# Half of the expert scatter issued inside the down products, and half of its adds issued ahead of the scatter weights

## The chip, the core and the metric

One core of one Trainium2 chip runs the whole program. The metric is device time in microseconds (us), the median of several executions. Engines: PE is TensorE, DVE is VectorE, ACT is ScalarE, POOL is GpSimd, SP is SyncE, which here issues the weight transfers.

## The reference

One decoder layer over T = 320 tokens (256 of a prompt, 8 sequences of 8) with D = 1024: adaLN modulation, an input projection, two gated linear recurrences, their merge and output projection, and then a mixture of experts, top 4 of 32. In float32:

```python
h2 = rmsnorm(x, n2) * (1 + sc2) + sh2
top_v, top_i = lax.top_k(h2 @ r_w + r_b, 4)      # softmax over the four
for e in range(32):
    gu = h2 @ w_gu[e] + b_gu[e]                  # w_gu[e]: 1024 x 2048
    gate, up = min(gu[:, :1024], 7), clip(gu[:, 1024:], -7, 7)
    act = (up + 1) * (gate * sigmoid(1.702 * gate))
    out += combine[:, e:e+1] * (act @ w_dn[e] + b_dn[e])   # w_dn[e]: 1024 x 1024
y = rmsnorm(x + gt2 * out, final_g)
```

## The kernel before

Everything ahead of the experts is as it was and is not touched. Each expert's tokens are cut into items of at most 32 tokens (CAP). In the profiled execution there are 56 items for 32 experts, each expert with one, two or three. PE, ACT and DVE each run a loop over items; SP runs a loop over experts and only issues transfers.

**Weights.** An expert has 12 slots of 1 MB: slots 0 to 7 hold rows of w_gu, slots 8 to 11 two blocks of w_dn each. Slots 3 to 11 have one buffer in the ring, so the transfer for expert e waits until the last item of expert e-1 has used the slot (L434, on slot_used; L431 on gu_ready; L433 on dn_ready). Slots 0 to 2 have two buffers (ring for even experts, late for odd ones). Transfers go out in the order of the slots.

**One item on PE** (item, L835 to L872), in the order of its queue:

1. bias (L842, four matmuls) and the gate/up products (L848, eight blocks k of four matmuls, each for 32 of the array's columns, written 128*32 in the profile), block k after slot k has landed;
2. gather(i + 1) (L802), which picks the next item's tokens by a selection matrix;
3. scatter of the first half (L818, n = 0 to 3): it takes the down result of the item before (dng) and its scatter weights (SelWT) and spreads the 32 rows over the 320 tokens. Each n is one matmul on 32 rows of the array (32*128), and the four of a half lie on the four row groups; they go to banks 4, 5, 6, 7;
4. two transposes of the activations (L858) after act_ready, and two of the gathered tokens (L809);
5. scatter of the second half (n = 4 to 7), to the same four banks. Matmul n waits until DVE has added bank n - 4 into yacc (pe.wait_ge on summed, L817);
6. the wait for act_copied, the down products (L867, eight blocks of four matmuls, 128*32), then three transposes of the next scatter weights (L824, flip_weights).

A float32 matmul is two instructions on PE, so a group of four matmuls stands as 8.

**One item on DVE** (L1508 to L1521): select (L1496), the clamped activation (L1512 to L1516, which sets act_ready), three operations for the scatter weights SelW (L1518), one for the bias selection (L1501), and then add_scattered, eight adds of 320 columns, one for each bank (L1506).

**One item on ACT** (L1090 to L1099): sigmoid (L1092), copies of the gathered tokens (L1080), of the flipped activations actT (L1095, sets act_copied), of the flipped tokens (L1084), of the down result dng (L1098, after dn_ready) and of the scatter weights (L1088).

After the last item PE scatters the last down result (L925) and DVE scales yacc and adds it to xT (L1537 to L1550).

Of the kernel before, what the change touches and what calls it, by code (L numbers as in the profile page):

```python
# [48 lines left out]
GRP = P // CAP  # L49
# [119 lines left out]
def build(nc, a):  # L169
    ctx = ExitStack()  # L170
    with ctx:
# [46 lines left out]
        def cut(at, n):  # L218
            return bigv[:, at:at + n]
# [3 lines left out]
        def units(ap, n):  # L223
            return ap.rearrange("p (u t) -> p u t", u=n)
# [4 lines left out]
                 k=units(cut(3 * HT, HT), 4), kd=units(cut(4 * HT, HT), 4), qs=units(cut(5 * HT, HT), 4)),  # L229
# [10 lines left out]
        def C(name, rows=P):  # L240
            at, n = CONST_COLS[name]
            return consts[0:rows, at:at + n]
# [118 lines left out]
        def item_slot(s):  # L361
            return (SLOT0 + s) % NSLOT
# [4 lines left out]
        def item_buffer(s, odd):  # L367
            return late[:, s * SLOT:(s + 1) * SLOT] if odd and s < NAHEAD else ring[:, item_slot(s), :]

        def pair(n):  # L370

            return ring[:, n % NSLOT, :].rearrange("p (k c) -> p k c", k=2)
# [7 lines left out]
        FEATURES = [2 * (n % GRP) + n // GRP for n in range(DC)]  # L380
# [138 lines left out]
        def _(pe):  # L519
# [266 lines left out]
            def chunk(k):  # L786

                at = (k % 2) * P + (k // 2) * CAP
                return slice(at, at + CAP)

            def part(g):
                return slice(CAP * g, CAP * g + CAP)

            def columns(g):
                return slice(HALF * g, HALF * g + HALF)

            def gather(j):

                pe.wait_ge(sel_ready, j + 1)
                for p in range(3):  # L800
                    for g in range(GRP):
                        last = mm(banks[0][part(g), 0:HALF], Sel[:, p, :], h2tok[:, p, columns(g)],  # L802
                                  start=(p == 0), stop=(p == 2), tile_position=(0, CAP * g))
                last.then_inc(gathered, 1)

            def flip_gathered(j):
                pe.wait_ge(gtok_copied, j + 1)
                for x in range(2):
                    last = nc.tensor.transpose(banks[0][:, HALF + x * P:HALF + (x + 1) * P], gtok[:, x * P:(x + 1) * P], ident)  # L809
                last.then_inc(gtok_flipped, 1)  # L810

            def scatter(i, fills):

                for n in fills:
                    x, g = n // GRP, n % GRP
                    if n >= GRP:
                        pe.wait_ge(summed, i * 8 + (n - GRP + 2))  # L817
                    mm(banks[SCATTER[n]][:, 0:T], dng[part(g), x * P:(x + 1) * P], SelWT[part(g), :],  # L818
                       start=True, stop=True, tile_position=(CAP * g, 0)).then_inc(scattered, 1)

            def flip_weights(j):
                pe.wait_ge(selw_ready, j + 1)
                for p, (t0, tn) in enumerate(TILES):
                    last = nc.tensor.transpose(banks[3][:, t0:t0 + tn], SelW[0:tn, p, :], ident[0:tn, 0:tn])  # L824
                last.then_inc(selw_flipped, 1)

            def wait_weights(s, pairs, odd):
                if s >= NAHEAD:
                    pe.wait_ge(slot_landed[item_slot(s)], pairs * 32 + (16 * odd + item_landed_count(s)))
                elif odd:  # L830
                    pe.wait_ge(late_landed[s], pairs * 16 + 16)
                else:
                    pe.wait_ge(slot_landed[item_slot(s)], pairs * 16 + item_landed_count(s))

            def item(i, pairs, odd):  # L835

                pe.wait_ge(h2g_copied, i + 1)
                pe.wait_ge(bsel_ready, i + 1)
                out = banks[1][:, :].rearrange("p (m c) -> p m c", m=2)
                bias = bgu.rearrange("p (m c) -> p m c", m=2)  # L840
                for g in range(GRP):
                    mm(out[part(g), :, :], bsel[0:96, :], bias[0:96, :, columns(g)], start=True, stop=False,  # L842
                       tile_position=(0, CAP * g))
                for k in range(DC):
                    wait_weights(k, pairs, odd)
                    w = item_buffer(k, odd).rearrange("p (m c) -> p m c", m=2)
                    for g in range(GRP):
                        last = mm(out[part(g), :, :], h2g[:, chunk(k)], w[:, :, columns(g)], start=False, stop=(k == DC - 1),  # L848
                                  tile_position=(0, CAP * g))
                    last.then_inc(gu_ready if k == DC - 1 else slot_used, 1)  # L850
                gather(i + 1)
                pe.wait_ge(dn_copied, i + 1)
                pe.wait_ge(selw_copied, i + 1)
                pe.wait_ge(summed, i * 8 + 1)
                scatter(i, range(GRP))
                pe.wait_ge(act_ready, i + 1)
                for x in range(2):
                    last = nc.tensor.transpose(banks[2][:, x * P:(x + 1) * P], actb[:, x * P:(x + 1) * P], ident)  # L858
                last.then_inc(act_flipped, 1)
                flip_gathered(i + 1)  # L860
                scatter(i, range(GRP, 2 * GRP))
                pe.wait_ge(act_copied, i + 1)
                for k in range(DC):
                    if k % 2 == 0:
                        wait_weights(DC + k // 2, pairs, odd)
                    for g in range(GRP):
                        last = mm(banks[2][part(g), HALF:2 * HALF], actT[:, chunk(k)],  # L867
                                  pair(item_slot(DC + k // 2))[:, k % 2, columns(g)],
                                  start=(k == 0), stop=(k == DC - 1), tile_position=(0, CAP * g))
                    if k % 2:  # L870
                        last.then_inc(dn_ready if k == DC - 1 else slot_used, 1)
                flip_weights(i + 1)  # L872

            X = NI
# [38 lines left out]
            with pe.Fori(0, E // 2) as pairs:  # L913
                e = pairs * 2
                n0, n1, n2 = first_item(e), first_item(e + 1), first_item(e + 2)
                with pe.Fori(n0, n1) as i:
                    item(i, pairs, False)
                with pe.Fori(n1, n2) as i:
                    item(i, pairs, True)
# [198 lines left out]
        def _(dve):  # L1118
# [371 lines left out]
            def col(tab, p, j):  # L1490
                return tab[:, p, j:j + 1] if isinstance(j, int) else tab[:, p, ds(j, 1)]

            def select(j):

                for p in range(3):
                    ins = TS(Sel[:, p, :], C("slot_no")[:, 0:CAP], col(posI, p, j), None, ALU.is_equal)  # L1496
                ins.then_inc(sel_ready, 1)

            def select_bias(j):
                c = OHI[0:96, j:j + 1] if isinstance(j, int) else OHI[0:96, ds(j, 1)]  # L1500
                TS(bsel[0:96, :], ones[0:96, 0:CAP], c, None, ALU.mult).then_inc(bsel_ready, 1)  # L1501

            def add_scattered(i):
                for n, f in enumerate(FEATURES):
                    dve.wait_ge(scattered, i * 8 + (n + 1))
                    TT(yacc[:, f, :], yacc[:, f, :], banks[SCATTER[n]][:, 0:T], ALU.add).then_inc(summed, 1)  # L1506

            def item(i):  # L1508
                dve.wait_ge(gathered, i + 1)
                select(i + 1)  # L1510
                dve.wait_ge(gu_ready, i + 1)
                TS(gbuf, banks[1][:, 0:HALF], LIMIT, None, ALU.min).then_inc(gate_clamped, 1)  # L1512
                step(TS(ubuf, banks[1][:, HALF:2 * HALF], -LIMIT, LIMIT, ALU.max, ALU.min))  # L1513
                step(STT(ubuf, ubuf, 1.0, gbuf, ALU.add, ALU.mult))  # L1514
                dve.wait_ge(swish_ready, i + 1)
                TT(actb, ubuf, sbuf_, ALU.mult).then_inc(act_ready, 1)  # L1516
                for p in range(3):
                    ins = TS(SelW[:, p, :], C("slot_no"), col(posI, p, i), col(wI, p, i), ALU.is_equal, ALU.mult)  # L1518
                ins.then_inc(selw_ready, 1)
                select_bias(i + 1)  # L1520
                add_scattered(i)  # L1521

            PER_ITEM = 2
            n0 = S.n
# [1 line left out]
            with dve.Fori(0, count) as i:  # L1526
                S.base = i * PER_ITEM
                item(i)
                assert S.n == n0 + PER_ITEM
# [72 lines left out]
```

## Time and profile before

| what | value |
|---|---|
| time, median of 3 runs | 1543.33 us (1541.24 to 1546.66) |
| the profiled execution's own time | 1542.54 us |
| its span, first to last instruction | 1540.7 us |
| PE busy | 1397.3 us, 91% |
| DVE busy | 523.0 us, 34% |
| ACT busy | 275.0 us, 18% |
| mean granted TensorE clock | 0.932 |
| first item starts / last item's L824 ends | 460.88 / 1518.10 us |

The row of the span and the row of the time differ by 1.8 us that lie outside the first and the last instruction. The items take 1057 of the 1541 us. A busy PE is not a PE at its peak: the ends of matmuls are modelled and the clock changes.

### The profile page before, as it was taken

The page shows a single profiled execution, that of the slowest core. Times are in us where ns is not written, and L with a number is a line of the kernel's source. Part 1 is how long each engine was busy: PE and PEld are TensorE (multiplying, and loading weights), DVE is VectorE, ACT ScalarE, POOL GpSimd, SP SyncE. Part 2 cuts the span into 40 slices and gives each one's busy share as a digit, 9 for nine tenths or more (in the row PEclk, how much of TensorE's full clock was granted, in tenths as well). Part 3 has the DMA queues.
Part 4 walks back from the last instruction along what each step waited for, and adds up shares of the span by engine and source line. Part 5 has one row for each costly group of instructions (what it writes and reads, how often), then busy time and mean ns, then how long its engine had stood idle before and what let it go on. Part 6 is the DMA issues. An engine that isn't in the chain of part 4 may idle for free.

```text
span 1540.7 us, 30155 instructions
## 1 busy us (share of the span) xinstructions
PE 1397.3 (91%) x11837; PEld 668.9 (43%) x11838; DVE 523.0 (34%) x1490; ACT 275.0 (18%) x517; POOL 22.8 (1%) x38
## 2 busy tenths in 40 slices
PE   5999999999969997988798999898999789899996
PEld 2656666666743442433242443333344223344443
DVE  3133342333463341323242433333334223333335
ACT  2120021010021121211111222121221112122222
POOL 0000010000000000000000000000000000000000
PEclk9999989788979999999798999999999989999998
DMA  9777342013348899999999989997899999985760
GB/s 391 304 289 272 140 166 109 16 51 132 91 178 330 350 388 418 410 408 420 416 411 410 388 356 386 417 412 287 327 379 375 417 418 412 410 358 208 291 245 34
DMA packets 87448, 470.77 MB, mean 306 GB/s; under 512 B 7984, under 2 KB 8000, under 8 KB 51360
## 3 DMA queue, kind: packets, MB, share of 16 engines
q1 hardware_dynamic: 84416, 460.68, 73.8%
q0 software_dynamic: 2432, 7.75, 1.9%
q10 hardware_dynamic: 576, 2.00, 0.3%
q8 instruction: 17, 0.28, 0.1%
q14 instruction: 7, 0.06, 0.0%
HBM read 465.56 MB, written 4.85 MB: 305 GB/s over the span
## 4 chain that ended last, share of the span: by engine, by line
PE 70%; DMA 15%; DVE 8%; issue 4%; SPq 2%; DVEq 1%; ACT 0%
PE bank L848 21%; PE bank L867 12%; PE bank L600 11%; DMA ring<-in_exp_w_gu 8%; PE bank L818 7%; DMA ring<-in_exp_w_dn 6%; PE bank L732 2%; PE bank L747 2%; SPq L442 2%; PE bank L598 2%; PE bank L824 2%; DVE gates L1506 1%; DVE big L1514 1%; DVE big L1518 1%; DVE big L1513 1%
## 5 line engine op out<-in xcount | busy, mean ns | idle before, releaser
L848 PE MATMUL bank<-ring,big 128*32 128x512 f32 x2840 | 351.0, 633 | 49.1 <-DMA ring<-in_exp_w_gu 48.8
L1512 DVE TENSOR_SCALAR big<-bank 128x256 f32<-128x256 f32 x56 | 23.8, 425 | 705.3 <-PE bank L848 705.3
L867 PE MATMUL bank<-ring,big 128*32 128x256 f32 x3584 | 221.8, 401 | 3.8 <-DMA ring<-in_exp_w_dn 3.8
L848 PEld LDWEIGHTS bank<-ring,big 128*32 128x32 f32 x2840 | 84.5, 113 | 287.2 <-issue 169.4
L818 PE MATMUL bank<-big 32*128 32x320 f32 x912 | 161.9, 481 | 26.6 <-DVE gates L1506 25.0
L1506 DVE TENSOR_TENSOR gates<-gates,bank 128x320 f32<-128x320 f32 x448 | 182.7, 477 | 1.5 <-PE bank L818 1.5
L600 PE MATMUL bank<-late,ring 128*128 128x320 f32 (+1 forms) x592 | 177.4, 461 | 3.9 <-DVE late L1166 3.1
L867 PEld LDWEIGHTS bank<-ring,big 128*32 128x32 f32 x3584 | 115.6, 115 | 107.5 <-issue 39.8
L600 PEld LDWEIGHTS bank<-late,ring 128*128 128x128 f32 (+1 forms) x592 | 117.3, 201 | 68.8 <-issue 27.5
L818 PEld LDWEIGHTS bank<-big 32*128 32x128 f32 x912 | 84.9, 183 | 82.6 <-DVE gates L1506 38.3
L1092 ACT ACTIVATE big<-big 128x256 f32<-128x256 f32 x56 | 23.4, 417 | 452.3 <-DVE big L1512 452.3
L848 PE MATMUL bank<-late,big 128*32 128x512 f32 x744 | 87.0, 598 | 3.9 <-DMA late<-in_exp_w_gu 3.9
L802 PE MATMUL bank<-vtok,big 128*32 128x256 f32 x1368 | 88.5, 395 | 1.4 <-DVE big L1451 1.4
L1098 ACT ACTIVATE big<-bank 128x256 f32<-128x256 f32 x56 | 21.5, 384 | 335.3 <-PE bank L867 335.3
L802 PEld LDWEIGHTS bank<-vtok,big 128*32 128x32 f32 x1368 | 44.3, 115 | 64.3 <-issue 44.9
L1092 ACT ACT_TABLE_LOAD x56 | 71.8, 1283 | 1.1 <-issue 0.2
L1518 DVE TENSOR_SCALAR big<-consts,big 128x128 f32<-128x128 f32 x168 | 47.8, 341 | 0.1
L842 PE MATMUL bank<-big 96*32 96x512 bf16 x224 | 22.6, 392 | 22.2 <-issue 22.2
L848 PEld LDWEIGHTS bank<-late,big 128*32 128x32 f32 x744 | 22.0, 109 | 46.5 <-issue 36.0
L732 PE MATMUL bank<-gates,ring 128*128 128x320 f32 x128 | 37.6, 459 | 0.6 <-DVE gates L1361 0.6
L824 PE MATMUL bank<-consts,big 128*128 128x128 f32 x171 | 36.9, 293 | 0.0
L548 PE MATMUL bank<-ring,Sst 128*32 128x512 f32 x192 | 25.5, 672 | 12.3 <-DVE Sst L1127 6.5
(265 smaller groups left out, 945.2 us busy)
## 6 DMA issues: line engine op xcount, KB each, us to landing
ring<-in_exp_w_gu SPq DMA_DIRECT2D x208, 1024.0 KB, 11.4
ring<-in_exp_w_dn SPq DMA_DIRECT2D x128, 1024.0 KB, 11.2
late<-in_exp_w_gu SPq DMA_DIRECT2D x48, 1024.0 KB, 15.4
ring<-in_ada_w SPq DMA_DIRECT2D x24, 1024.0 KB, 20.6
ring<-in_w_in SPq DMA_DIRECT2D x20, 1024.0 KB, 9.7
ring<-in_w_out SPq DMA_DIRECT2D x4, 1024.0 KB, 7.4
ring<-in_w_in SPq DMA_DIRECT2D x4, 528.0 KB, 10.1
late<-in_state_hgrn POOLq DMA_DIRECT2D x4, 512.0 KB, 7.6
```

The source lines that it names most:

```text
L442: sp.dma_start(dst, src).then_inc(late_landed[s] if ahead and odd else slot_landed[item_slot(s)], 16)
L598: ins = mm(b[0:tn, :], hT[:, k, t0:t0 + tn], wts, start=(k == 0), stop=(k == DC - 1))
L600: ins = mm(b[0:w, 0:T], wts, hT[:, k, :], start=(k == 0), stop=(k == DC - 1))
L732: ins = mm(b[:, 0:T], pair(s0 + k // 2)[:, k % 2, f * P:(f + 1) * P], gates[:, 4 * bi + k, :], start=(k == 0), stop=(k == H - 1))
L802: last = mm(banks[0][part(g), 0:HALF], Sel[:, p, :], h2tok[:, p, columns(g)], start=(p == 0), stop=(p == 2), tile_position=(0, CAP * g))
L818: mm(banks[SCATTER[n]][:, 0:T], dng[part(g), x * P:(x + 1) * P], SelWT[part(g), :], start=True, stop=True, tile_position=(CAP * g, 0)).the ...
L824: last = nc.tensor.transpose(banks[3][:, t0:t0 + tn], SelW[0:tn, p, :], ident[0:tn, 0:tn])
L848: last = mm(out[part(g), :, :], h2g[:, chunk(k)], w[:, :, columns(g)], start=False, stop=(k == DC - 1), tile_position=(0, CAP * g))
L867: last = mm(banks[2][part(g), HALF:2 * HALF], actT[:, chunk(k)], pair(item_slot(DC + k // 2))[:, k % 2, columns(g)], start=(k == 0), stop= ...
L1092: A(sbuf_, gbuf, ACT.Sigmoid, scale=ALPHA).then_inc(swish_ready, 1)
L1506: TT(yacc[:, f, :], yacc[:, f, :], banks[SCATTER[n]][:, 0:T], ALU.add).then_inc(summed, 1)
L1518: ins = TS(SelW[:, p, :], C("slot_no"), col(posI, p, i), col(wI, p, i), ALU.is_equal, ALU.mult)
```

## The change

The second half of the scatter leaves its place ahead of the down products and is issued after block k = 3 of the eight. add_scattered is cut in two: the adds of n = 0 to 3 come directly after the activation, ahead of the scatter weights; the adds of n = 4 to 7 stay at the end. No operation is added or removed, and the semaphores count as before.

```diff
                 last.then_inc(act_flipped, 1)
                 flip_gathered(i + 1)
-                scatter(i, range(GRP, 2 * GRP))
                 pe.wait_ge(act_copied, i + 1)
                 for k in range(DC):
...
                     if k % 2:
                         last.then_inc(dn_ready if k == DC - 1 else slot_used, 1)
+                    if k == 3:
+                        scatter(i, range(GRP, 2 * GRP))
                 flip_weights(i + 1)
...
-            def add_scattered(i):
-                for n, f in enumerate(FEATURES):
+            def add_scattered(i, x):
+                for n in range(GRP * x, GRP * x + GRP):
+                    f = FEATURES[n]
                     dve.wait_ge(scattered, i * 8 + (n + 1))
                     TT(yacc[:, f, :], yacc[:, f, :], banks[SCATTER[n]][:, 0:T], ALU.add).then_inc(summed, 1)
...
                 TT(actb, ubuf, sbuf_, ALU.mult).then_inc(act_ready, 1)
+                add_scattered(i, 0)
                 for p in range(3):
                     ins = TS(SelW[:, p, :], C("slot_no"), col(posI, p, i), col(wI, p, i), ALU.is_equal, ALU.mult)
                 ins.then_inc(selw_ready, 1)
                 select_bias(i + 1)
-                add_scattered(i)
+                add_scattered(i, 1)
```

## Rows read from the trace of the kernel before

**Rows 1.** The page: chain of work that ended last, by engine.

```profile
PE 70%; DMA 15%; DVE 8%; issue 4%; SPq 2%; DVEq 1%; ACT 0%
```

**Rows 2.** The stretches of items: length, busy of each engine, PEclk, DMA share, GB/s.

```profile
564.25:625.10 60.85, 52.16 (x538) 20.91 (x538) 18.53 (x57) 10.69 (x21) 0.00 (x0) 0.94 0.97 398
...
686.17:777.18 91.01, 76.30 (x718) 27.75 (x718) 24.59 (x76) 14.26 (x28) 0.00 (x0) 0.87 1.01 414
...
1179.32:1270.22 90.90, 74.82 (x718) 27.49 (x717) 24.78 (x76) 14.26 (x28) 0.00 (x0) 0.89 0.98 399
1270.22:1330.97 60.75, 53.27 (x538) 21.37 (x538) 18.44 (x57) 10.69 (x21) 0.00 (x0) 0.92 1.01 414
460.88:564.25 103.37, 99.05 (x1075) 42.82 (x1076) 37.02 (x114) 19.67 (x40) 0.00 (x0) 0.97 0.89 360
...
1061.49:1179.32 117.83, 112.06 (x1255) 48.83 (x1255) 43.02 (x133) 24.95 (x49) 0.00 (x0) 1.00 0.82 333
1330.97:1518.10 187.13, 179.44 (x1970) 77.70 (x1969) 70.51 (x214) 39.21 (x77) 0.00 (x0) 0.98 0.65 264
```

**Rows 3.** Timeline of one item: start, us, engine, line, operation, [idle before <- what ended it].

```profile
906.92 0.40 PE L842 MATMUL bank<-big 96*32 96x512 bf16 x4
...
907.15 7.04 PE L848 MATMUL bank<-ring,big 128*32 128x512 f32 x64
...
915.41 0.82 PE L818 MATMUL bank<-big 32*128 32x320 f32 x8
915.52 0.42 DVE L1516 TENSOR_TENSOR big<-big 128x256 f32<-128x256 f32 x1
...
915.86 0.85 DVE L1518 TENSOR_SCALAR big<-consts,big 128x128 f32<-128x128 f32 x3
916.16 0.20 PEld L858 LDWEIGHTS bank<-consts,big 128*128 128x128 f32 x2 [0.44 <-DVE big L1516]
...
916.64 0.38 ACT L1095 ACTIVATE big<-bank 128x256 f32<-128x256 f32 x1 [0.70 <-PE bank L858]
916.78 3.26 DVE L1506 TENSOR_TENSOR gates<-gates,bank 128x320 f32<-128x320 f32 x8
...
917.30 1.99 PE L818 MATMUL bank<-big 32*128 32x320 f32 x8 [0.48 <-DVE gates L1506]
...
919.23 3.66 PE L867 MATMUL bank<-ring,big 128*32 128x256 f32 x64
...
922.82 0.64 PE L824 MATMUL bank<-consts,big 128*128 128x128 f32 x3
...
923.39 0.40 PE L842 MATMUL bank<-big 96*32 96x512 bf16 x4
```

**Rows 4.** Timeline of PE alone, from just before the first scatter.

```profile
915.09 0.39 PE L802 MATMUL bank<-vtok,big 128*32 128x256 f32 x4
```

**Rows 5.** Transfers: one SP issue in order of time.

```profile
568.29 3.76 SPq L442 DMA_DIRECT2D ring<-in_exp_w_gu  x5
```

**Rows 6.** Chain of waits over the span: down products, first and last longer one.

```profile
507.75 5.28 PE bank L867 x64
...
1446.37 5.28 PE bank L867 x64
```

**Rows 7.** Windows before and in one of those down products (columns as Rows 2).

```profile
503.90:507.70 3.80, 3.32 (x27) 1.89 (x23) 3.77 (x13) 1.04 (x3) 0.00 (x0) 1.00 1.00 423
508.10:511.40 3.30, 3.30 (x38) 1.69 (x32) 0.83 (x4) 0.00 (x0) 0.00 (x0) 0.50 0.99 417
```

**Rows 8.** Timeline of PE in an item whose weights lag.

```profile
752.91 1.93 PE L848 MATMUL bank<-ring,big 128*32 128x512 f32 x8 [0.55 <-DMA ring<-in_exp_w_gu]
```

**Rows 9.** Timeline after the last item.

```profile
1514.71 0.69 DVE L1537 TENSOR_TENSOR gates<-gates,modT 128x512 f32<-128x512 f32 x1
...
1518.62 0.68 DVE L1541 TENSOR_TENSOR xT<-xT,gates 128x512 f32<-128x512 f32 x1
...
1519.80 0.22 DVE L1545 TENSOR_TENSOR gates<-bank,modT 128x64 f32<-128x64 f32 x1 [0.50 <-PE bank L818]
```

## The prediction

> **What bounds the kernel now.** I read the chain of waits first: PE has 70% of it and the DMA 15% [rows 1]. The items take 1057 of the 1541 us, and the change touches nothing else, so the question is in which items PE sets the pace and in which the weights do. For that I cut the items into stretches and took the windows of each [rows 2]. Eight stretches contain an expert with a single item: six of three items, 60.75 to 61.07 us long (first and last shown), and two of four items, 91.01 and 90.90 us. In these the DMA engines are 0.97 to 1.02 busy at about 400 to 414 GB/s. The other four stretches hold 30 items (6, 6, 7 and 11; three shown), where the DMA share is 0.65 to 0.93 and an item takes 16.47 us from one L842 to the next [rows 3]. There PE, and what it waits for, sets the pace.
>
> Inside such an item the timeline shows where PE does little. The first scatter takes 0.82 us for four matmuls side by side. The second takes 1.99 us for the same four, because each waits for an add (eight adds in 3.26 us, 0.41 apart), and the first add begins only after SelW and the bias selection, at 916.78. Meanwhile actT was ready at 917.02 (916.64 + 0.38), and the down products begin at 919.23 [rows 3].
>
> **The change in a PE-bound item.** All operations remain, 8 scatters and 8 adds.
>
> *Moved out:* the down products now wait for act_copied alone. ACT's copy ends at 917.02, and a semaphore takes about 0.05 us (the first add ends near 917.25, the scatter starts at 917.30), so they start at 917.08: 2.15 us earlier.
>
> *Moved in:* the scatter after k = 3. From the start of one group to the start of a scatter of the other tile shape took 0.32 us (L802 at 915.09, L818 at 915.41) [rows 3, 4]; the unpaced scatter takes 0.82; after the old one L867 started 0.07 before its modelled end; and the step to the next group that would have been there anyway, 0.22 (3.59 us for 16 groups), is deducted [rows 3]. That is 0.85, and I take 0.89 for the slower first step after a switch. The waits inside are satisfied and I cost them at nothing: L848 too waits for a slot before each of its eight blocks, and its 64 instructions run in 7.04 us without a gap [rows 3]. Their cover is that PE is busy with products while its queue runs ahead.
>
> *Are the waits really satisfied?* The first scatter's results are there at about 916.2 (915.41 + 0.80), so DVE stands idle 0.3 us after L1516 and then adds from 916.27 to 917.94. The scatter inside starts at 917.08 + 1.79 + 0.1 = 918.97. Its first matmul needs the first add (916.75), its last one the fourth (917.94): 1.0 us to spare. Queued on DVE behind the new waits are SelW (0.85, now ready near 918.8 instead of 916.7) and the bias selection (near 919.0). flip_weights wants SelW at 921.56 and the next L842 wants the bias near 922.1, so both are hidden by some 2.7 us. The second adds run from about 919.8 to 921.4, then select; the gather needs that 7 us later. ACT's order is unchanged. On SP the release of slots 8 and 9 comes 2.15 us earlier, and everything later 1.26 us; no wait is added and nothing stands behind one.
>
> So L824 starts at 917.08 + 3.59 + 0.89 = 921.56 instead of 922.82. An item saves 2.15 - 0.89 = **1.26 us** and takes 15.21.
>
> *Bounds of the insertion.* Below: without any cost of the switch, 0.65 (saves 1.5). Above: if the four matmuls follow one another at the old pace, 0.1 + 1.93 = 2.03 (saves 0.12). The nearest row is the first scatter, whose waits were satisfied and whose shape is the same, hence 0.89.
>
> A rule speaks against the change. The Trainium skill, TensorEngine Tiling (Array Packing), Key Properties, says that a change of tiling mode drains the engine, and the new order has one change of mode more. The rows put a switch at 0.1 us over a plain step (0.32 against 0.22). If the drain meant waiting for the last matmul's full 0.39 us, the insertion would be 0.96 and the saving 1.19 us: 2 us less over 30 items, which the range holds.
>
> **Where it does not arrive.** In the eight stretches the stream is already full. Each begins when the last item of an expert releases slot 3, about 4 us after its start (564.25 in [rows 2], 568.29 in [rows 5]), and ends when the last slot of the expert after the single one has landed. Faster PE work inside changes neither. I cost them at zero gain: 26 items x 1.26 = 33 us that are not received.
>
> In the PE-bound stretches a two-item expert comes close to the stream as well. One more expert adds 91.0 - 60.9 = 30.1 us; a three-item stretch less one expert leaves 30.75, and two new items take 30.42 [rows 2]. At seven changes of expert with no loop step of PE between them, about 0.3 us is lost: 2.2 us.
>
> **The clock.** Nine of the 56 down products take 5.28 instead of 3.59 us in the chain (first and last shown of the four in PE-bound stretches) [rows 6]. The granted clock in one of them was 0.50, that is 1.2 instead of 2.4 GHz, and just before PE had issued only 27 instructions in 3.8 us: transposes, the wait for the first add, the paced scatter [rows 7]. Those 3 sparse us shrink to about one. I expect these drops to vanish: 4 x 1.69 = 6.8 us (the other five fall in stream-bound stretches and are free).
>
> Against it: at the exit of a stream-bound stretch the down products now wait for their slots themselves (a slot lands every 2.5 us, 30.1 / 12, and has 0.9 us of products, so PE is a third busy). In such phases before, the clock stood at half for long, and a block took 1.93 us instead of 1.04 [rows 8]. If the last blocks and the next item's first ones meet such a spell, an exit costs about 1.7 us. I take half of the eight exits: 6.8 us given back; bounds 0 and 13.5.
>
> **The tail.** DVE ends its last adds now 0.7 us before the end of L824 instead of 3.4. Behind them stand L1537 to L1541: from 1514.71 to 1519.30. L1545 started at 1519.80 [rows 9], so 0.5 of the shift of 2.65 us is hidden and **2.1 us** are added.
>
> **Sum** against the profiled execution's 1542.5 us (span 1540.7 and 1.8 around it; the median of the runs, 1543.3, is 0.8 above): -30 x 1.26 = -37.8; +2.2 stream; -6.8 clock; +6.8 exits; +2.1 tail. Together -33.5, that is **1509 us**.
>
> **Rivals.**
>
> A. *The inserted scatter is not concurrent.* Four matmuls with a wait each could go one after another, 2.03 us. For: every scatter of this form with waits in the trace ran at 0.41 us each. Against: there the adds set exactly this pace. Saves 0.12 x 30 = 3.6 us, clock 6.8 gained, exits not worse, tail +2.1: about 1534. Halfway (insertion 1.4): about 1522. Decides from an insertion over 1.2.
>
> B. *Slower: the clock falls in the down products of every item.* A switch of tile shape in the middle with matmuls on 32 rows could leave a sparse phase in each item. For: half clock did follow the old scatter nine times. Against: 47 times it did not, and the phase is now denser. Price 1.69 for the products and 0.4 for the scatter against 1.26 saved: +0.8 x 30 = 25, tail 2: about 1569. It turns to slower from about three items in five.
>
> C. *The clock gets worse at the exits and the short drops stay.* Exits 13.5, no 6.8 won: about 1522.
>
> D. *The stream hides it anyway.* If the whole were stream-bound, nothing would change: 1543. Against it the DMA share of 0.65 to 0.93 in four stretches [rows 2].
>
> E. *Everything goes well:* no cost at the exits, insertion 0.65: -4 and -6.8, about 1498.
>
> **Chances.** Forecast, 1502 to 1516: 0.50; E 0.14; C 0.14; A with its halfway case 0.15 (fully 0.05); B 0.04; D 0.03. The range leaves out B, D, the full A and the lower part of E: 1496 to 1530. A measurement of this kernel tells about 0.3% (5 us) from nothing. Faster: all but B, D and a little of A, 0.92; same 0.03; slower 0.05.
>
> **What would show it.** Right: L867 starts some 0.05 us after ACT's L1095 ends in every PE-bound item, the second L818 takes 0.8 us between two parts of L867, the period is 15.2, and PE no longer idles before L818 for DVE's adds; the eight stretches keep 60.8 and 91.0 us. Wrong: a second L818 of 1.5 us or more (A); down products of over 7 us with a clock of 0.5 (B); stretches longer than before (C). The prediction fails if the down products find another late partner or if PE pays more than 0.9 us for the interruption.

## The result and the profile after

The changed kernel takes 1508.21 us (median of 4 runs, 1502.62 to 1510.14) against 1544.99 us for the kernel before beside it: a ratio of 0.9757, 95% interval 0.9721 to 0.9793. It is faster by 2.4%, and the forecast was 1509. A second series (changed_again below) gave 1507.68 us and 0.9777.

The profiled execution is the lowest of the four runs, 1502.6 us with a span of 1500.8. Its first item starts at 456.60 instead of 460.88 us. Nothing was changed ahead of the items, and in the other profiles of this study that start lies between 457.4 and 463.0 whatever the kernel, so 4.3 of its 39.9 us are not the change's. The items themselves go from 1057.2 to 1019.2 us, 38.0 less, and the tail after them from 22.6 to 25.0, 2.4 more.

The timeline of one item after (columns as in [rows 3]; lines have moved by a few, L866 was L867, L1096 was L1095, L1508 was L1506, L1518 was L1516):

```profile
915.15 0.82 PE L818 MATMUL bank<-big 32*128 32x320 f32 x8
915.25 0.42 DVE L1518 TENSOR_TENSOR big<-big 128x256 f32<-128x256 f32 x1
...
915.90 0.44 PE L858 MATMUL bank<-consts,big 128*128 128x128 f32 x2
915.99 1.68 DVE L1508 TENSOR_TENSOR gates<-gates,bank 128x320 f32<-128x320 f32 x4 [0.31 <-PE bank L818]
...
916.38 0.39 ACT L1096 ACTIVATE big<-bank 128x256 f32<-128x256 f32 x1 [0.69 <-PE bank L858]
...
916.82 1.93 PE L866 MATMUL bank<-ring,big 128*32 128x256 f32 x32 [0.26 <-ACT big L1096]
917.59 0.85 DVE L1521 TENSOR_SCALAR big<-consts,big 128x128 f32<-128x128 f32 x3
...
918.68 0.82 PE L818 MATMUL bank<-big 32*128 32x320 f32 x8
...
919.43 2.21 PE L866 MATMUL bank<-ring,big 128*32 128x256 f32 x32
919.52 1.68 DVE L1508 TENSOR_TENSOR gates<-gates,bank 128x320 f32<-128x320 f32 x4 [0.93 <-PE bank L818]
...
920.56 0.59 PEld L866 LDWEIGHTS bank<-ring,big 128*32 128x32 f32 x16 [0.55 <-DMA ring<-in_exp_w_dn]
```

This answers to [rows 3]. The down products start 0.05 us after ACT's copy ends (916.38 + 0.39) and wait 0.26 us for it. The second scatter, 1.99 us long before, is 0.82 long and lies between two parts of the products. DVE idles 0.31 us before its first four adds. A PE-bound item takes 15.21 us in place of 16.47. The item shown is the last of its stretch and took 15.48: the second part of its products is 2.21 us long instead of 1.93, because a slot of w_dn landed late (PEld at 920.56).

The windows of the stretches, same items as in [rows 2]:

```profile
core 0: us, PE busy (x) PEld busy (x) DVE busy (x) ACT busy (x) POOL busy (x), PEclk, DMA share, GB/s
554.45:616.55 62.10, 51.16 (x539) 17.90 (x538) 19.00 (x57) 10.69 (x21) 0.00 (x0) 0.92 0.99 405
677.38:768.18 90.80, 71.14 (x718) 23.16 (x717) 25.33 (x76) 14.26 (x28) 0.00 (x0) 0.89 1.01 415
...
1153.83:1244.77 90.94, 71.35 (x718) 23.01 (x718) 25.32 (x76) 14.26 (x28) 0.00 (x0) 0.89 1.00 412
1244.77:1305.54 60.77, 51.65 (x539) 18.07 (x538) 19.00 (x57) 10.69 (x21) 0.00 (x0) 0.89 1.01 414
456.60:554.45 97.85, 92.65 (x1074) 36.29 (x1074) 37.99 (x114) 19.67 (x40) 0.00 (x0) 0.98 0.92 375
1044.63:1153.83 109.20, 105.00 (x1255) 42.01 (x1254) 44.33 (x133) 24.95 (x49) 0.00 (x0) 1.00 0.86 349
1305.54:1475.84 170.30, 165.05 (x1970) 65.53 (x1969) 69.92 (x207) 39.20 (x77) 0.00 (x0) 1.00 0.71 290
```

The stretches with a single-item expert keep their length: 90.80 and 90.94 where 91.01 and 90.90 stood, 60.77 where 60.75 stood. Two have grown, the first by 1.25 us and the one from 922.14 to 983.81 (not shown) by 0.80. The other four gave all of the gain, 39.7 us (510.1 to 470.4). One of them, from 829.10 to 922.14 (not shown, 93.04 us), now has a DMA share of 1.00 itself. PE's busy share went down in the stream-bound ones: the saved work became waiting for weights.

The last items' tail answers to [rows 9]:

```profile
1475.14 0.69 DVE L1540 TENSOR_TENSOR gates<-gates,modT 128x512 f32<-128x512 f32 x1
1475.20 0.64 PE L824 MATMUL bank<-consts,big 128*128 128x128 f32 x3
...
1476.66 0.82 PE L818 MATMUL bank<-big 32*128 32x320 f32 x8 [0.82 <-ACT big L1089]
1479.04 0.69 DVE L1544 TENSOR_TENSOR xT<-xT,gates 128x512 f32<-128x512 f32 x1
1479.76 0.23 DVE L1548 TENSOR_TENSOR gates<-bank,modT 128x64 f32<-128x64 f32 x1
```

PE's last scatter ends at 1477.5 and DVE takes it up only at 1479.76, after its own queue. Before, it waited 0.50 us for PE at this place; now PE is ready 2.3 us earlier than DVE.

### The profile page after: what moved, and what is told of

Its sections match the earlier page's. It is cut to its first block, busy times and chain, and to the rows that moved or that the text cites. A ratio compares the mean times of both kernels' runs of the same rounds, so it can differ in the third digit from the quotient of the medians.

```text
span 1500.8 us, 30155 instructions
## 1 busy us (share of the span) xinstructions
PE 1336.0 (89%) x11837; PEld 604.8 (40%) x11838; DVE 533.0 (36%) x1490; ACT 275.0 (18%) x517; POOL 22.8 (2%) x38
## 4 chain that ended last, share of the span: by engine, by line
PE 68%; DMA 20%; SPq 6%; DVE 2%; issue 2%; ACT 1%; DVEq 0%
PE bank L848 19%; DMA ring<-in_exp_w_dn 17%; PE bank L600 12%; PE bank L866 10%; SPq L442 6%; PE bank L818 4%; PE bank L802 4%; PE bank L732 2%; PE bank L747 2%; PE bank L598 2%; DMA ring<-in_exp_w_gu 2%; PE bank L824 2%; DMA ring<-in_ada_w 1%; ACT big L1096 1%; PE bank L548 1%
## 5 line engine op out<-in xcount | busy, mean ns | idle before, releaser
L848 PE MATMUL bank<-ring,big 128*32 128x512 f32 x2840 | 358.1, 643 | 47.1 <-DMA ring<-in_exp_w_gu 47.1
L866 PE MATMUL bank<-ring,big 128*32 128x256 f32 x3584 | 221.6, 383 | 33.3 <-DMA ring<-in_exp_w_dn 18.5
L1508 DVE TENSOR_TENSOR gates<-gates,bank 128x320 f32<-128x320 f32 x448 | 188.3, 483 | 74.4 <-PE bank L818 74.4
L848 PEld LDWEIGHTS bank<-ring,big 128*32 128x32 f32 x2840 | 85.0, 114 | 295.9 <-issue 169.0
L600 PE MATMUL bank<-late,ring 128*128 128x320 f32 (+1 forms) x592 | 174.0, 454 | 3.1 <-DVE late L1167 3.1
L866 PEld LDWEIGHTS bank<-ring,big 128*32 128x32 f32 x3584 | 102.4, 109 | 137.0 <-DMA ring<-in_exp_w_dn 34.9
L1093 ACT ACTIVATE big<-big 128x256 f32<-128x256 f32 x56 | 23.4, 417 | 479.5 <-DVE big L1514 479.5
L848 PE MATMUL bank<-late,big 128*32 128x512 f32 x744 | 91.5, 613 | 20.0 <-DMA late<-in_exp_w_gu 20.0
L818 PE MATMUL bank<-big 32*128 32x320 f32 x912 | 96.1, 483 | 3.8 <-DVE xT L1551 3.0
L818 PEld LDWEIGHTS bank<-big 32*128 32x128 f32 x912 | 37.3, 184 | 51.4 <-issue 47.5
L842 PE MATMUL bank<-big 96*32 96x512 bf16 x224 | 22.6, 392 | 23.1 <-issue 23.1
L824 PE MATMUL bank<-consts,big 128*128 128x128 f32 x171 | 36.8, 293 | 0.0
## 6 DMA issues: line engine op xcount, KB each, us to landing
ring<-in_ada_w SPq DMA_DIRECT2D x24, 1024.0 KB, 20.6
```

Of the source, the lines that this page charges most:

```text
L600: ins = mm(b[0:w, 0:T], wts, hT[:, k, :], start=(k == 0), stop=(k == DC - 1))
L1093: A(sbuf_, gbuf, ACT.Sigmoid, scale=ALPHA).then_inc(swish_ready, 1)
```

## The experiments

Each profile was cut into the same stretches (from one L842 to the next). "Eight" are the stream-bound stretches together, 26 items, "four" the PE-bound ones, 30 items; both come from the one profiled execution. The item is one inside an expert whose weights do not lag. Each ratio is to executions of the kernel before beside that run, whose medians lie between 1542.67 and 1544.99 us.

| kernel | median us | ratio to before, 95% | item us | eight us | four us |
|---|---|---|---|---|---|
| before | 1544.99 | 1 | 16.47 | 547.1 | 510.1 |
| changed | 1508.21 | 0.9757 (0.9721 to 0.9793) | 15.21 | 548.9 | 470.4 |
| adds_ahead_only | 1521.72 | 0.9846 (0.9816 to 0.9877) | 15.96 | 547.5 | 489.5 |
| scatter_inside_only | 1507.89 | 0.9751 (0.9714 to 0.9788) | 15.21 | 549.1 | 472.0 |
| no_second_scatter | 1504.73 (one run) | | 14.32 | 551.3 | 468.2 |
| scatter_split | 1531.99 | 0.9912 (0.9886 to 0.9937) | 16.07 | 547.7 | 499.2 |
| scatter_after_k1 | 1504.81 | 0.9745 (0.9724 to 0.9765) | 15.21 | 547.8 | 469.4 |
| scatter_after_k5 | 1513.31 | 0.9800 (0.9763 to 0.9838) | 15.21 | 547.8 | 476.8 |
| k1_late_adds | 1509.81 (one run) | | 15.61 | 546.9 | 479.5 |
| light_stream_before | 1439.43 | 0.9328 (0.9300 to 0.9356) | 16.47 | 443.1 | 513.4 |
| light_stream_after | 1361.01 | 0.8805 (0.8775 to 0.8835) | 15.21 | 407.0 | 466.5 |
| light_k5 | 1381.70 (one run) | | 15.21 | 417.4 | 474.5 |
| changed_again | 1507.68 | 0.9777 (0.9748 to 0.9806) | 15.21 | 548.0 | 470.8 |
| k1_again | 1504.77 | 0.9747 (0.9720 to 0.9774) | 15.21 | 547.8 | 470.6 |

### The two halves of the change

**adds_ahead_only**, the scatter back at its old place:

```diff
                 flip_gathered(i + 1)
+                scatter(i, range(GRP, 2 * GRP))
                 pe.wait_ge(act_copied, i + 1)
...
-                    if k == 3:
-                        scatter(i, range(GRP, 2 * GRP))
```

> Only the DVE half of the change: the adds of n = 0 to 3 ahead of SelW, the scatter of the second half at its old place. Theory of the sum: the four adds start 0.5 us earlier and still pace the scatter, so a PE-bound item takes 16.47 - 0.5 = 15.97 us; 30 such items give 15 us, about 1528, and about 1521 if the short half-clock spells go too. Rival 1, the adds' place is worth nothing without the scatter's move: 1543. Rival 2, it is the main part: under 1515.

PE's timeline of one item of adds_ahead_only:

```profile
907.31 0.82 PE L818 MATMUL bank<-big 32*128 32x320 f32 x8
908.06 0.44 PE L858 MATMUL bank<-consts,big 128*128 128x128 f32 x2
908.34 0.38 PE L809 MATMUL bank<-consts,big 128*128 128x128 f32 x2
908.69 1.99 PE L818 MATMUL bank<-big 32*128 32x320 f32 x8
910.61 3.66 PE L867 MATMUL bank<-ring,big 128*32 128x256 f32 x64
```

The scatter still takes 1.99 us, paced by the adds, but starts 0.63 us after the transposes (908.06 to 908.69) where it took 1.14 before. The item is 15.96 us, as the sum said, and the half-clock down products of the four stretches are gone as well: 20.6 us less in them, 15.3 from 30 x 0.51 and 6.8 from the clock (four of 1.69 us), less 1.4 us that its first item took beyond the sum. The time, 1521.7, is the expectation's with both.

**scatter_inside_only**, the eight adds behind SelW as before:

```diff
                 TT(actb, ubuf, sbuf_, ALU.mult).then_inc(act_ready, 1)
-                add_scattered(i, 0)
                 for p in range(3):
...
                 select_bias(i + 1)
+                add_scattered(i, 0)
                 add_scattered(i, 1)
```

> Only the PE half of the change: the scatter after k = 3, all eight adds after SelW and the bias selection as before. Theory of the sum: the first add starts at 0.5 us later than in the full change but the fourth still ends 0.5 us before the scatter inside wants to start, so the item takes 15.21 us as with both halves, and the time is that of the full change, 1502 to 1510, with the second adds in the same place. Rival: the adds' place carries a part of the gain; then the scatter inside is paced (over 0.9 us long) and the item takes 15.5 us or more, over 1515.

1507.89 us and 15.21 us an item: with the scatter after k = 3, the DVE half of the change adds nothing that can be measured. The full change is not the sum of its halves (22 and 36 us). Moving the scatter makes the DVE half unneeded; the reverse does not hold, for with the adds ahead alone the scatter is still paced and the item takes 15.96 us.

**k1_late_adds** looks for the place where the DVE half does count: `if k == 1` for the scatter, adds as in scatter_inside_only.

> Scatter after k = 1 with all eight adds after SelW and the bias selection as before the change. It asks when the DVE half of the change counts. Theory: the scatter is wanted 1.0 us after the down products start, the fourth add ends 0.35 us later than that, so the last of its four matmuls waits, and the item takes 15.5 to 15.6 us against 15.21 with the adds ahead (profile of scatter_after_k1). Rival: 15.21 here too, the adds' place never counts.

```profile
887.62 1.07 PE L866 MATMUL bank<-ring,big 128*32 128x256 f32 x16 [0.25 <-ACT big L1096]
888.62 1.22 PE L818 MATMUL bank<-big 32*128 32x320 f32 x8
889.76 2.80 PE L866 MATMUL bank<-ring,big 128*32 128x256 f32 x48
```

Here the scatter is 1.22 us long, 0.40 more than unpaced, and the item 15.61. The adds' place is a matter of slack: worth 0.4 us an item after k = 1 and nothing after k = 3.

### What the insertion costs

**no_second_scatter** leaves the second half out of the loop (the contribution of n = 4 to 7 for all items but the last) with its adds, and counts four a loop:

```diff
-                    if k == 3:
-                        scatter(i, range(GRP, 2 * GRP))
...
-                add_scattered(i, 1)
```

> The changed kernel without the second half of the scatter in the item loop and without its four adds (the contribution of n = 4 to 7 is left out for all items but the last). It prices the insertion by itself. Theory: a PE-bound item takes 15.21 - 0.89 = 14.32 us and the down products run through in 3.59 us to L824. If the insertion were cheap (0.65), 14.55; if a full drain is paid twice (1.1), 14.1. Two-item experts are then stream-bound throughout, so the time falls by less than 10 us.

```profile
906.60 3.66 PE L866 MATMUL bank<-ring,big 128*32 128x256 f32 x64 [0.26 <-ACT big L1094]
910.19 0.64 PE L824 MATMUL bank<-consts,big 128*128 128x128 f32 x3
910.76 0.40 PE L842 MATMUL bank<-big 96*32 96x512 bf16 x4
```

The item is 14.32 us, so the inserted scatter costs 15.21 - 14.32 = 0.89 us, the value that the sum took. The one time measured is only some 3 us below the changed kernel's, no more than executions of one kernel differ by: of 30 x 0.89 = 27 us the four stretches show 2.2. At 14.32 us two items (28.6) are shorter than an expert's 30.1 us of transfers, so the stream of weights takes nearly all of the rest.

**scatter_split** issues n = 4, 5 after k = 3 and n = 6, 7 after k = 5.

```diff
                     if k == 3:
-                        scatter(i, range(GRP, 2 * GRP))
+                        scatter(i, range(GRP, GRP + 2))
+                    if k == 5:
+                        scatter(i, range(GRP + 2, 2 * GRP))
```

> The changed kernel with the second scatter cut in two: n = 4, 5 after k = 3 and n = 6, 7 after k = 5. It has two more changes of tile shape and only two matmuls side by side. Theory, the price is the latency of a float32 matmul pair plus two switches, not its columns: each part costs about the 0.87 us of the whole, so the insertion is 1.7 us, the item 16.0 us, and the time 20 to 25 us above the changed kernel (about 1530). Rival, the price goes with the number of matmuls: 0.33 x 2 + 2 x 0.2, about 1.06 us, item 15.4, about 1510.

```profile
913.95 1.93 PE L866 MATMUL bank<-ring,big 128*32 128x256 f32 x32 [0.26 <-ACT big L1098]
915.82 0.81 PE L818 MATMUL bank<-big 32*128 32x320 f32 x4
916.55 1.07 PE L866 MATMUL bank<-ring,big 128*32 128x256 f32 x16
917.55 0.81 PE L818 MATMUL bank<-big 32*128 32x320 f32 x4
918.29 1.07 PE L866 MATMUL bank<-ring,big 128*32 128x256 f32 x16
```

Two matmuls take 0.81 us where four took 0.82. The item is 16.07, so two insertions cost 16.07 - 14.32 = 1.75 us, 0.87 each. The price is that of an interruption, not of its matmuls; all four belong in one. The Trainium skill, TensorEngine Tiling (Array Packing), Key Properties, says that a change of tiling mode drains the engine and that tiles work independently of each other. The rows agree with both: the scatter starts 0.06 us before the modelled end of the products ahead of it and the next products 0.08 us before the scatter's, while 16 groups of one shape follow each other every 0.22 us (3.59 us in all) with matmuls of 0.38 us; and two matmuls cost what four do. The ends are modelled, but the prices, 0.87 and 0.89 us, come from starts alone.

### Whether the stream takes the rest

**light_stream_before** and **light_stream_after** cut the transfers into the ring to half, in both kernels alike:

```diff
-                        src = a["exp_w_gu"][0, ds(e, 1), s * P:(s + 1) * P, :].rearrange("a p c -> p (a c)")
-                        dst = item_buffer(s, odd)
+                        w = SLOT if ahead and odd else D
+                        src = a["exp_w_gu"][0, ds(e, 1), s * P:(s + 1) * P, 0:w].rearrange("a p c -> p (a c)")
+                        dst = item_buffer(s, odd)[:, 0:w]
...
-                        src = a["exp_w_dn"][0, ds(e, 1), k * P:(k + 2) * P, :].rearrange("a (k p) c -> p (a k) c", p=P)
-                        dst = pair(item_slot(s))
+                        src = a["exp_w_dn"][0, ds(e, 1), k * P:(k + 1) * P, :].rearrange("a p c -> p (a c)")
+                        dst = ring[:, item_slot(s), 0:D]
```

> The kernel before, with the transfers of the expert weights into the ring cut to half (slots 0 to 7: the first 1024 of 2048 columns, slots 8 to 11: the first of two blocks; the three early buffers stay whole), so a part of the products works on old weights. All instructions of the engines stay. Theory: every item becomes PE-bound, 56 x 16.47 and 15 steps of the expert loop at 1.3 us, with half-clock spells about 958 us for the items and 1443 us in all. Rival, the stream is not what holds the eight stretches: 1520 or more.

> The changed kernel with the same cut of the transfers, a part of the products on old weights. Theory: now all 56 items receive the saving of 1.26 us instead of 30: 70 us less than the cut kernel before, and the short half-clock spells (about 15 us) go as well, so about 1360 us and a difference of 70 to 85 us. Rival, the 26 items of the eight stretches lose their saving for another reason than the stream: a difference of about 40 us as between the uncut kernels.

All items, before and after, with the stream cut:

```profile
459.70:1416.18 956.48, 911.16 (x10024) 395.97 (x10024) 347.12 (x1069) 197.76 (x390) 0.00 (x0) 0.98 0.62 227
```

```profile
462.87:1336.33 873.46, 840.91 (x10024) 337.22 (x10024) 354.54 (x1062) 197.88 (x390) 0.00 (x0) 1.00 0.67 250
```

The items differ by 83.0 us and the medians by 78.4, in place of 38.0 and 36.8 with the whole stream. 56 x 1.26 is 70.6; seven down products at half clock before and none after give 7 x 1.69 = 11.8 more, and the rest, 0.6, lies in the first item. The eight stretches alone, which moved by less than 2 us with the whole stream, now give 36.1. So it is the stream that kept the saving of their 26 items. The mean clock over the items after is 1.00; only the first item began at half clock (0.58 over its first 6 us).

### Where inside the products

**scatter_after_k1** and **scatter_after_k5** change the 3 in `if k == 3` to 1 and 5.

> The changed kernel with the second scatter after k = 1 instead of k = 3. Theory: it wants to start 1.03 us after the down products do (918.1 in the item of the profile before), the fourth add ends at 917.94, so it still does not wait; the item stays 15.21 us, and the tail after the last item gets 0.86 us shorter. Time within 0.2% of the changed kernel. Rival: the adds now pace it, item 15.4 or more, time 5 us above.

> The changed kernel with the second scatter after k = 5 instead of k = 3. Theory: the item stays 15.21 us, the tail gets 0.86 us longer, slot 9 is released as late as before relative to k and slot 10 earlier; in stream-bound items the scatter lies in a gap of the weights either way. Time within 0.2% of the changed kernel. Rival: the scatter of an item whose weights lag now comes closer to the last slot and lengthens the eight stretches by up to 0.9 us each: 7 us.

After k = 1 the item stays 15.21 us and the scatter 0.82: the fourth add is just in time. Its tail was expected to be 0.86 us shorter and is 0.4 shorter. After k = 5 the item stays 15.21 too, and the tail, expected to be 0.86 us longer, is 0.1 longer. The median is 5 us above the changed kernel's; the intervals of the two overlap, but the stretches show where time goes, and both the theory and the rival of the expectation are wrong: the eight stretches did not grow (547.8 us), the four did (476.8 against 470.4, and 470.8 in changed_again). PE's timeline of scatter_after_k5 at a step to the next pair of experts, and after it the changed kernel's at the same step:

```profile
1140.69 0.82 PE L818 MATMUL bank<-big 32*128 32x320 f32 x8
1141.44 1.07 PE L866 MATMUL bank<-ring,big 128*32 128x256 f32 x16
1142.44 0.64 PE L824 MATMUL bank<-consts,big 128*128 128x128 f32 x3
1144.70 0.40 PE L842 MATMUL bank<-big 96*32 96x512 bf16 x4 [1.62 <-issue]
1144.92 8.75 PE L848 MATMUL bank<-ring,big 128*32 128x512 f32 x64
```

```profile
1136.78 0.64 PE L824 MATMUL bank<-consts,big 128*128 128x128 f32 x3
1138.62 0.40 PE L842 MATMUL bank<-big 96*32 96x512 bf16 x4 [1.21 <-issue]
```

The gap of the loop step is 1.62 us instead of 1.21, and the gate/up products behind it take 8.75 instead of 7.04: the clock was at 0.50 for a spell.

**light_k5** takes the weights out of this question: light_stream_after with `if k == 5`.

> The kernel with the cut stream (a part of the products on old weights) and the second scatter after k = 5. It asks what the lateness of the scatter costs where no weight lags. Theory from the profile of scatter_after_k5: items inside an expert keep 15.21 us; the step to the next pair of experts takes 1.7 us instead of 1.28, because PE's sequencer reaches the register work of the loop later, and at that gap the clock falls to 0.5 for a spell in several of the 15 steps, 1.7 us each. So the items take 873.5 + 15 x 0.43 = 880 us plus 5 to 15 spells, 888 to 905. Rival: the longer times of scatter_after_k5 came from the weights; then 873 to 875.

Its items take 891.9 us against 873.5. Every one of the 15 loop steps costs about 1.7 us where light_stream_after has 1.28 (16.90 and 16.49 us to the next item, less 15.21), and seven of them are followed by gate/up products of 8.5 to 8.8 us: 15 x 0.41 + 7 x 1.69 = 18.0, and the first item took 0.5 more, which is the whole difference (18.5). No weight lagged, so the lateness of the scatter itself did it. scatter_split shows the same with two matmuls after k = 5 instead of four: its loop steps cost 1.7 us too (17.76 to the next item, less 16.07), and five of them are followed by gate/up products of 8.75 us. I read the longer gap so: PE's register work for the next loop begins later, because it stands behind the scatter's waits. No run took the waits alone away, so this stays argued.

### Once more, side by side

> The changed kernel once more, beside k1_again on the same chip. Theory: 1502 to 1510, 0.973 to 0.979 of the kernel before; no half-clock spell in a PE-bound item.

> Scatter after k = 1 with the adds ahead, once more. Theory: the same items as the changed kernel (15.21 us) and a tail some 0.4 us shorter, so 0 to 3 us below the changed kernel; not separable from it if the ratios to the kernel before overlap. Rival: the 3.4 us between the medians so far are real, and the ratio stays at 0.9745 or below with a gap to the changed kernel's interval.

On one chip, with five runs each: 1507.68 us (1507.58 to 1512.85) and, after k = 1, 1504.77 (1502.46 to 1505.85). The ratios to the kernel before, 0.9777 and 0.9747, have overlapping intervals, as in the first series. k = 1 is clearly faster than the kernel before, and its medians were below the changed kernel's by about 3 us both times. Side by side, all five of its times lie below all five of the changed kernel's; in the first series they lie within them. But in the two profiled executions side by side, 3.3 us apart, 2.7 us lie ahead of the first item (462.98 against 460.26 us), where both kernels are the same. The items differ by 0.4 us (1018.8 against 1018.4; in the first series by 2.1) and the tail by 0.2 (24.07 against 23.85; in the first series 24.96 against 24.54). So a gain of k = 1 over k = 3 that comes from its place is not shown.

## Why the prediction was right

**What bounds.** Right. Six of the eight stretches kept 60.8 and 91.0 us, two grew by about 1 us, and cutting the stream set their saving free. Rival D fails by the four stretches, which gave 39.7 us.

**The item.** Right: 0.89 us for the insertion (no_second_scatter), 1.26 saved, 15.21 an item. That it is right to the hundredth is luck, because the rows added up to 0.85 and the last 0.04 had no row. The satisfied waits cost nothing that the rows show. Rival A fails: the inserted scatter is 0.82 us long, four side by side.

**Are the waits satisfied.** Right with 1.0 us to spare after k = 3; k1_late_adds shows what happens when 0.35 us too little is left: the scatter takes 0.40 us longer. The prediction did not say that the DVE half of the change is idle at this place; scatter_inside_only shows it.

**The stream inside the four stretches** was set too small: 2.2 us against about 4.1 read from the items after. Five of the seven changes of expert cost 0.16 to 0.27 us, near the 0.3 worked out, but the two of the first stretch 1.4 and 1.5. The sum also had no term for the first item, which has a clock below full at its start and saved 0.5 instead of 1.26.

**The short spells of half clock.** Right: nine down products of 5.3 us before, none at half clock in the PE-bound items after, and none of 56 with the stream cut. Rival B fails. The sparse phase before the fall was sparse in matmuls, not empty: PE was never idle for more than half a us in it [rows 3, 7]. The other 47 items before had the same phase without a fall; what set the nine apart is open.

**The exits** were the term of the sum that was mis-sized most: 6.8 us forecast, and no exit of this profile paid any of it. In the stalled items (those of more than 20 us) the clock did spend more time at half, 102 us instead of 85, but the spells ended before the exit. The window of one such item's gate/up and of the rest of it:

```profile
586.45:604.70 18.25, 10.35 (x61) 1.33 (x60) 0.00 (x0) 1.72 (x2) 0.00 (x0) 0.81 1.01 420
604.70:616.55 11.85, 10.63 (x120) 4.48 (x120) 6.33 (x19) 1.84 (x5) 0.00 (x0) 0.86 1.03 415
```

The next item's gate/up products took 7.04 us in all eight cases. The eight stretches did grow by 1.7 us (547.14 to 548.85), but by another cause. The two that grew follow a PE-bound stretch whose last item had already waited for weights, and more was loaded in them: 62.10 us at 405 GB/s is 25.2 MB, 60.85 us at 398 GB/s was 24.2, about one slot more. That is an estimate from the windows: the stream came into these stretches about one slot behind. The mechanism of the forecast exists all the same: in the profile of scatter_inside_only one exit of the eight met such a spell and paid 1.7 us.

```profile
831.29 1.07 PE L866 MATMUL bank<-ring,big 128*32 128x256 f32 x16 [1.48 <-DMA ring<-in_exp_w_dn]
832.30 0.64 PE L824 MATMUL bank<-consts,big 128*128 128x128 f32 x3
832.87 0.43 PE L842 MATMUL bank<-big 96*32 96x512 bf16 x4
833.09 8.74 PE L848 MATMUL bank<-ring,big 128*32 128x512 f32 x64
```

It is a matter of where the spell falls. Of the 56 exits in the seven profiles with the whole scatter inside the products and the whole stream, this is the only one, where the forecast took half. Rival C fails. The half of rival E that said no cost at the exits came true, its cheaper insertion did not; its 4 us for that insertion do not follow from 30 x 0.24 = 7.2 either.

**The tail.** 2.1 us forecast, 2.4 measured, by the mechanism named.

**The whole.** Term by term, in us:

| term | forecast | in the profiles |
|---|---|---|
| 30 items x 1.26 | -37.8 | -37.8 |
| the first item | none | +0.8 |
| stream inside the four stretches | +2.2 | +4.1 |
| short spells of half clock | -6.8 | -6.8 |
| the eight stretches (forecast: exits) | +6.8 | +1.7 |
| tail | +2.1 | +2.4 |
| sum | -33.5 | -35.6 |

Between the medians it is -36.8. The two large terms, the item and the spells, were right by their mechanism. That the sum came so close is in part luck: 5.1 us too much for the exits stood against 3.0 too little for the rest.

## What to carry to other kernels

Work that waits for another engine costs least inside a dense run of its own engine, once its waits have had time to be satisfied, and not too near the end of the run: after k = 5 the items kept their 15.21 us, but the step of the outer loop grew. It then pays one interruption (here 0.9 us for two or four small matmuls alike), so give it one place and everything in it.

Before pricing a saving per item, separate the items that the stream of weights paces: here 26 of 56 kept nothing, and taking a further 0.89 us out of each item brought 2.2 us in the four stretches.

A change can have a redundant half. Run the halves alone before both are kept, and ask how much slack each leaves.

## What the runs showed of the hardware that I had not expected

Two 32-row float32 matmuls of 320 columns on different row groups take 0.81 us and four take 0.82.

TensorE's clock fell to half without any long idle time. Before the change it fell in nine of 56 down products, each time after a phase of about 3 us of transposes and matmuls issued one at a time (besides the spells in which PE waited for weights). With the scatter after k = 5 and the stream cut (light_k5) it fell at seven of 15 loop steps, where a scatter, 1.07 us of products, three transposes and a gap of 1.6 us come together; with the scatter after k = 3 and a gap of 1.2 us, at none.

Where the scatter stands in PE's loop body changed the cost of the outer loop's step: 1.28 us with it after k = 1 or 3 or left out, 1.7 with all or half of it after k = 5. The cause was not isolated.
